# First head's probabilities turned by VectorE squares and DMA instead of TensorE, in the dilated branch and in three tiles of the forgetting branch

## The reference

```python
def forgetting_attention(q, k, v, log_f):      # branch A: 8 heads of 64
    ...
        logits = jnp.einsum('bqhd,bkhd->bhqk', qb, k) * scale
        logits = logits + (cb[..., :, None] - c[..., None, :])   # c = cumsum(log_f)
        logits = jnp.where(kpos[None, :] <= qpos[:, None], logits, -jnp.inf)
        p = jax.nn.softmax(logits, axis=-1)
        return jnp.einsum('bhqk,bkhd->bqhd', p.astype(v.dtype), v)
```

## Time and profile before

| | before |
|---|---|
| median of 3 runs | 1376.3 us (1376.18 to 1376.54) |
| the profiled execution | 1376.36 us, span 1374.6 us |
| PE, PEld, DVE, ACT, POOL busy | 1352.1, 1102.6, 741.4, 659.3, 153.2 us |
| granted TensorE clock | 0.999 |
| dilated branch, 135.9 to 406.6 | PE 266.09, DVE 186.45, ACT 177.18 us busy |
| forgetting branch, 615.4 to 843.2 | PE 225.81, DVE 99.87, ACT 119.22 us busy |

### The profile page before, as it was taken

One profiled execution on the slowest core, in us unless ns is written; L12 is line 12 of the kernel. 1 busy time (PEld: TensorE's weight loads), 2 busy tenths in 40 slices (PEclk: granted clock), 3 DMA queues, 4 the chain that ended last, 5 costly groups with the idle time before them and its releaser, 6 DMA issues.

```text
span 1374.6 us, 20906 instructions
## 1 busy us (share of the span) xinstructions
PE 1352.1 (98%) x7882; PEld 1102.6 (80%) x7882; DVE 741.4 (54%) x1675; ACT 659.3 (48%) x1430; POOL 153.2 (11%) x259
## 2 busy tenths in 40 slices
PE   7999999999999999999999999999999999999998
PEld 6988877777878888887878777787888788888886
DVE  6568866666757874574434455533333354222634
ACT  7467766666644531115454565645454422113223
POOL 3123111102112000001101012100000030000100
PEclk9999999999999999999999999999999999999999
DMA  6055222212224322323303032211322242231522
GB/s 222 24 138 131 66 66 62 69 40 64 70 50 125 88 72 67 84 90 98 93 24 93 24 101 90 66 47 55 108 62 62 62 149 67 78 84 62 185 89 102
DMA packets 114677, 114.37 MB, mean 83 GB/s; under 512 B 10609, under 2 KB 96049, under 8 KB 114321
## 3 DMA queue, kind: packets, MB, share of 16 engines
q1 hardware_dynamic: 97824, 58.22, 15.7%
q0 software_dynamic: 16752, 54.82, 12.6%
HBM read 87.37 MB, written 21.45 MB: 79 GB/s over the span
## 4 chain that ended last, share of the span: by engine, by line
PE 92%; DVE 4%; ACT 2%; issue 1%; POOL 1%; DMA 0%; POOLq 0%; ACTq 0%; DVEq 0%
PE bank L1053 22%; PE bank L1055 22%; PE bank L1054 22%; PE bank L1199 6%; PE bank L1220 6%; PE slot L1187 6%; PE slot L1053 2%; PE slot L1054 2%; PE slot L1055 2%; DVE idle_out L1586 1%; PE slot L1161 1%; DVE slot L1771 1%; DVE qc L1714 1%; PE bank L1066 0%; ACT qc L1412 0%
## 5 line engine op out<-in xcount | busy, mean ns | idle before, releaser
L1053 PE MATMUL bank<-hs,w_hl 128*128 128x512 f32 x1088 | 431.8, 397 | 3.8 <-DVE qc L1714 2.9
L1055 PE MATMUL bank<-hs,w_hl 128*128 128x512 f32 x1088 | 424.3, 390 | 0.0
L1054 PE MATMUL bank<-hs,w_hl 128*128 128x512 f32 x1088 | 423.8, 390 | 0.0
L1053 PEld LDWEIGHTS bank<-hs,w_hl 128*128 128x128 f32 x1088 | 204.3, 188 | 48.9 <-issue 8.5
L1559 DVE TENSOR_TENSOR w_hl<-w_raw,w_hl 128x512 fp32r<-128x512 f32 (+1 forms) x168 | 113.5, 678 | 235.7 <-ACT w_hl L1284 234.1
L1055 PEld LDWEIGHTS bank<-hs,w_hl 128*128 128x128 f32 x1088 | 204.1, 188 | 43.6
L1054 PEld LDWEIGHTS bank<-hs,w_hl 128*128 128x128 f32 x1088 | 204.6, 188 | 39.6
L1284 ACT ACTIVATE w_hl<-w_raw 128x512 fp32r<-128x512 f32 (+1 forms) x168 | 103.9, 621 | 161.6 <-PE bank L1055 154.1
L1586 DVE TENSOR_SCALAR_CACHE_REDUCE idle_out<-score,state 128x768 uint8<-128x768 f32 (+3 forms) x140 | 115.3, 824 | 4.8
L1771 DVE CUSTOM_DVE_ANT_0 slot<-slot,score 128x128 f32<-128x128 f32 (+5 forms) x64 | 47.0, 786 | 75.4 <-PE slot L1187 75.4
L1468 ACT ACTIVATE idle_out<-score,state 128x896 bf16<-128x896 f32 x64 | 70.0, 1093 | 10.0 <-DVE state L1582 8.8
(11 more groups left out here) (320 smaller groups left out, 2211.2 us busy)
## 6 DMA issues: line engine op xcount, KB each, us to landing
w_raw<-in_w_in_dram SPq DMA_DIRECT2D x136, 256.0 KB, 2.9
merged_scratch<-ms POOLq DMA_DIRECT2D x16, 512.0 KB, 3.5
ms<-merged_scratch POOLq DMA_DIRECT2D x16, 512.0 KB, 3.8
xn<-in_x_dram SPq DMA_DIRECT2D x8, 512.0 KB, 6.8
iq_st<-iq_hl POOLq DMA_DIRECT2D x32, 128.0 KB, 2.8
w_raw<-in_w_o_dram SPq DMA_DIRECT2D x16, 256.0 KB, 3.7
v_scratch<-vtc POOLq DMA_DIRECT2D x6, 512.0 KB, 3.0
vc<-v_scratch POOLq DMA_DIRECT2D x24, 128.0 KB, 3.8
```

The source lines that it names most:

```text
L1053: pe.matmul(out_, wh, mh, start=start, stop=False)
L1054: pe.matmul(out_, wh, ml, start=False, stop=False)
L1055: return pe.matmul(out_, wl, mh, start=False, stop=stop)
```

## The change

The plan marks runs whose head 0 goes by DMA (`by_dma`): all but the last run of the dilated branch, and channels 0 to 2 of the forgetting branch. For these, ACT computes the exponentials of head 0 first, in a new step "square" that stands ahead of the turn; DVE transposes the 32x32 squares of PR in place; POOL stores them to DRAM and loads them in four DMAs into one of two new buffers PTQ; the turn has the blocks of head 1 alone; pv reads head 0 from PTQ. pv comes two steps behind as before in the dilated branch, and three behind in the marked channels of the forgetting branch. A marked run's turn is not cut by logits. The dilated branch's PT ring has two groups instead of four. ACT waits for the former square's store before it writes PR of head 0, and POOL for the pv two squares back before it loads.

```diff
+SQUARED = ("c", "a", )
+LAG = {"c": 2, "a": 3, "b": 2}
+PTS = {"c": 2, "a": 4, "b": 4}
...
+        by_dma = [r[0]["br"] in SQUARED and s + 1 < n and (r[0]["br"] == "c" or r[0]["ch"] + 1 < NCH["a"])
+                  for s, r in enumerate(runs)]
...
-            between = 1 <= s < n and runs[s - 1][0]["slots"] == 2
+            between = 1 <= s < n and runs[s - 1][0]["slots"] == 2 and not by_dma[s - 1]
...
-            if s >= 2:
+            late = LAG[runs[0][0]["br"]]
+            due = [r for r in range(max(s - 3, 0), min(s, n)) if r + (late if by_dma[r] else 2) == s]
+            for r in due:
                 pv = ring()
...
+            if s < n and by_dma[s]:
+                step("square", unit=runs[s][-1], n=len(squares), before=squares[-2] if len(squares) > 1 else None)
...
-                parts = [(x["b"], hh, c) for x in runs[s - 1] for hh in range(2) for c in range(x["W"] // P)]
+                parts = [(x["b"], hh, c) for x in runs[s - 1] for hh in range(1 if x["dma"] else 0, 2)
+                         for c in range(x["W"] // P)]
...
+        PTQ = {"c": [at(k, f"ptsc{k}", [P, 4, P]) for k in (58, 60)], "a": [at(k, f"ptsa{k}", [P, TB, P]) for k in (44, 76)]}
...
@@ POOL @@
+                elif kind == "square":
+                    pool.wait_ge(squared, n + 1)
+                    if n >= 2:
+                        pool.wait_ge(square_in, 64 * (n - 1))
+                    pool.dma_start(mid[0:W // P].rearrange("b p c -> p b c"),
+                                   PR[br][:, 0, 0:W].rearrange("p (b c) -> p b c", c=P)).then_inc(square_stored, 16)
+                    if a["before"] is not None:
+                        full(pool, a["before"]["pv"])
+                    pool.wait_ge(square_stored, 16 * (n + 1))
+                    for j in range(4):
+                        pool.dma_start(PTQ[br][n % 2][32 * j:32 * j + 32, 0:W // P, :].rearrange("a b (i c) -> a (b i) c", i=4),
+                                       mid[0:W // P, :, 32 * j:32 * j + 32].rearrange("b (i a) c -> a (b i) c", i=4)
+                                       ).then_inc(square_in, 16)
...
@@ PE, ahead of pv @@
+                        if a["dma"]:
+                            pe.wait_ge(square_in, 64 * (a["square"] + 1))
...
@@ ACT @@
+                elif kind == "square":
+                    if a["n"]:
+                        act.wait_ge(square_stored, 16 * a["n"])
+                    act.wait_ge(logit_ready, u["L"][0] + 1)
+                    for x in u["run"]:
+                        ins = A(PR[x["br"]][:, 0, x["col"]:x["col"] + x["W"]], slot_of(x, 0)[1], ACTF.Exp, bias=mx,
+                                scale=-1.0, accum_out=dn)
+                    ins.then_inc(slot_free if u["slots"] == 2 else single_exp, 1)
...
-                    for hh in range(2):
+                    for hh in range(1 if a["dma"] else 0, 2):
...
@@ DVE @@
+                elif kind == "square":
+                    v.transpose(PR[u["br"]][:, 0, 0:W], PR[u["br"]][:, 0, 0:W]).then_inc(squared, 1)
```

More of the change, by code:

```diff
@@ L55 @@
 RATE_B = 0.84
-PTS = 4
+SQUARED = ("c", "a", )
+LAG = {"c": 2, "a": 3, "b": 2}
+PTS = {"c": 2, "a": 4, "b": 4}
 RELUS = 3
@@ L223, in pair_run @@
         n = len(runs)
+        by_dma = [r[0]["br"] in SQUARED and s + 1 < n and (r[0]["br"] == "c" or r[0]["ch"] + 1 < NCH["a"])
+                  for s, r in enumerate(runs)]
+        for run, dma in zip(runs, by_dma):
+            for x in run:
+                x["dma"] = dma
         defer[0] = True
@@ L243, in turn @@
                 step("turn", unit=run[0], groups=groups)
-            between = 1 <= s < n and runs[s - 1][0]["slots"] == 2
+            between = 1 <= s < n and runs[s - 1][0]["slots"] == 2 and not by_dma[s - 1]
             if s < n and not between:
                 logits()
-            if s >= 2:
+            late = LAG[runs[0][0]["br"]]
+            due = [r for r in range(max(s - 3, 0), min(s, n)) if r + (late if by_dma[r] else 2) == s]
+            for r in due:
                 pv = ring()
-                for x in runs[s - 2]:
+                for x in runs[r]:
                     x["pv"] = pv
                     plan.append(("pv", x))
+            if s < n and by_dma[s]:
+                step("square", unit=runs[s][-1], n=len(squares), before=squares[-2] if len(squares) > 1 else None)
+                for x in runs[s]:
+                    x.update(square=len(squares), single=sum(y["slots"] == 1 for y in squares))
+                squares.append(runs[s][-1])
             if 1 <= s <= n:
-                parts = [(x["b"], hh, c) for x in runs[s - 1] for hh in range(2) for c in range(x["W"] // P)]
+                parts = [(x["b"], hh, c) for x in runs[s - 1] for hh in range(1 if x["dma"] else 0, 2)
+                         for c in range(x["W"] // P)]
                 groups = [dict(parts=parts[g0:g0 + 4]) for g0 in range(0, len(parts), 4)]
@@ L677, in hybrid_layer_kernel @@
         v_stored, v_in = sem("v_stored"), sem("v_in")
+        single_exp, squared, square_stored, square_in = sem("single_exp"), sem("squared"), sem("square_stored"), sem("square_in")
+        square_dram = [nc.dram_tensor(f"square_scratch_{i}", [TB, P, P], F32, kind="Internal").ap() for i in range(2)]
         v_dram = [nc.dram_tensor(f"v_scratch_{i}", [P, T], F32, kind="Internal").ap() for i in range(2)]
@@ L1213, in _ @@
                         first = a["b"] // 2 * 2
-                    at_part = {part: (grp["tp"] % PTS, j) for grp in a["groups"] for j, part in enumerate(grp["parts"])}
+                    at_part = {part: (grp["tp"] % PTS[a["br"]], j) for grp in a["groups"] for j, part in enumerate(grp["parts"])}
                     for c in range(n):
                         for hh in range(2):
-                            t, j = at_part[a["b"], hh, c]
+                            if a["dma"] and hh == 0:
+                                turned = PTQ[a["br"]][a["square"] % 2][:, a["col"] // P + c, :]
+                            else:
+                                t, j = at_part[a["b"], hh, c]
+                                turned = PT[a["br"]][:, t, j, :]
                             cols = slice(HD * hh, HD * hh + HD)
                             values = V["b"][:, c, :] if a["br"] == "b" else V[a["br"]][a["ch"] % 2][:, first + c, cols]
-                            ins = pe.matmul(bank[a["pv"][0]][cols, out], values, PT[a["br"]][:, t, j, :],
+                            ins = pe.matmul(bank[a["pv"][0]][cols, out], values, turned,
                                             start=c == 0, stop=c == n - 1)
@@ L1429, in _ @@
                         full(act, a["held"]["groups"][-1]["use"])
-                    for hh in range(2):
+                        if a["held"]["dma"] and not a["dma"]:
+                            act.wait_ge(square_stored, 16 * (a["held"]["square"] + 1))
+                    for hh in range(1 if a["dma"] else 0, 2):
                         act.wait_ge(logit_ready, a["L"][hh] + 1)
```

21 lines of the change are left out of this document (16 added, 5 removed).

## The result

The changed kernel takes 1411.0 us (median of 4, 1408.8 to 1416.1) against 1376.35: a ratio of 1.0257, interval 1.0228 to 1.0286. The profiled execution took 1408.83 us, span 1407.0. It is slower by 34.6 us, where 3 us less were forecast, and outside the range. Of all executions in this document one, of the kernel of e5, ran at a granted clock of 0.558 from end to end and took 2203.5 us, where the other four of that kernel took 1380.8 to 1388.7.

What follows compares the result with a forecast made beforehand. TensorE (PE), busy 1352.1 of 1374.6 us, was taken to bound the kernel. The sum was 1376.36 + 4.6 (dilated branch) - 7.6 (forgetting branch) = 1373.4 us, own range 1370 to 1377, full range 1363 to 1384.

Steps and rivals of the forecast that it cites:

- Part 1: Both branches: head 0's transposes leave PE, saving 11.0 us dilated and 12.8 us forgetting, less 0.7 us for logits.
- Part 2: Squares on DVE: 0.62 us each at 512 columns, delaying L1714 in the dilated branch by 11.4 us, covered in the forgetting branch.
- from 3.6 to about 19: Dilated stage: sign of being right, PE idle before projection matmuls rising to about 19 us, released by L1714.
- the nine: Dilated steps where DVE's delay reaches PE: two in each of channels 1 to 4, one in channel 5; 11.4 us.
- 11.4 - (11.0 - 4.2): Dilated branch sum: DVE delay less PE's saving outside the waiting steps, giving +4.6 us, slower.
- Part 3: DMA by POOL: cost 0 in the dilated branch; forgetting branch 3 us for last values, 1.5 us for late exponentials.
- Cost 0: Dilated branch: POOL's square DMA and the store ACT waits for, hidden within two steps (22 us), some 4 us left.
- 0.5 us more per step (ACT held by a count or by a late store): Dilated branch's slow bound: extra delay in the waiting steps, the branch losing 9 us instead of 4.6.
- the last channel's wait: Forgetting branch: PE waits 3 us (ends 0 and 4.5) for the last channel's values behind the last square's loads.
- The gating of the exponential: Forgetting branch: head 1's exponential, behind one turn's evictions, makes PE wait 0.3 us x 5 = 1.5 us (0 to 4).
- POOL's queue is late: Rival, both branches: square's store, awaited by ACT, stands behind former square's loads; 1390 us, about 1382 halfway; chance 0.29.
- Strided loads: Rival: square loads as slow as the skill's rule says, 40 squares each 5 us late, 200 us more; chance 0.01.

Runs made afterwards that it cites:

- e5: Changed kernel, dilated square behind the counts and first L1774, one buffer; forgetting channels 0 to 2 load values behind the next square's store: 1382.6 us, ratio 1.0052.
- e3: Changed kernel, DVE writing its squares straight into PTQ without DMA, values two runs behind in the forgetting branch too: 1374.0 us, ratio 0.9984.
- e7: Changed kernel with a second buffer for head 0's probabilities in the dilated branch: 1396.9 us, ratio 1.0139.
- e11: The same kernel as e5, run again for a profile at full clock: 1384.2 us, ratio 1.006.
- e6: Changed kernel, dilated: two buffers, square behind first read; forgetting: stores ahead of square and values' loads, last values' store ahead of last square's loads: 1365.0 us, ratio 0.9915.
- e8: Kernel before the change, plus three DVE transposes of an unused 128x512 buffer ahead of the counts in 24 dilated steps: 1404.6 us, ratio 1.0208.
- e12: Kernel before the change, plus one DVE transpose of an unused 128x512 buffer ahead of the counts in 24 dilated steps: 1383.2 us, ratio 1.0051.
- e9: e6 with dilated squares only in each channel's third and fourth run, the third's behind its step's last read: 1359.2 us, ratio 0.9877.

## Why the prediction was wrong, step by step

- **Part 1, right but for its size.** 72 and 180 turns are left, as said. At full clock PE's work falls by 265.9 - 256.4 = 9.5 us in the dilated stage (11.0 forecast) and 225.8 - 211.7 = 14.1 in the forgetting stage (12.1 net). (The "gross 24.1" of the text is 11.0 + 12.8 = 23.8; nothing rests on it.)
- **Part 2's duration of the square was right.** L1752 takes 0.711, 0.579 and 0.445 us for 512, 384 and 256 columns, and the next instruction starts 0.64, 0.50 and 0.37 us after it, against the 0.62, 0.49 and 0.35 of the text.
- **Part 2's mechanism was right, its price not.** Without DMA (e3) PE waits 19.0 us in the dilated stage, 15.1 more than before, and this is the "from 3.6 to about 19" of the prediction (1.4 of it, at 145.56, is in a step outside the nine). But the stage lengthened by 11.2 us, not 4.6. The sum "11.4 - (11.0 - 4.2)" has no term for PE's clock after the waits: 262.7 - 256.4 = 6.3 us. PE's smaller saving adds 1.5 us, waits 0.5 us shorter than forecast and fewer small gaps take 1.2 back.
- **Part 3 failed at "Cost 0" in the dilated branch, and this is the larger miss there.** The text holds that the store on which ACT's next exponential waits "is hidden with some 4 us left". The cover was counted from square to values; what stood uncovered was the path store, exponential, square, counts, L1774, with the values' move ahead of the store in POOL's queue. It costs 294.6 - 282.6 = 12.0 us (e7; 12.9 against e3), of which 5.7 is clock. The bound of "0.5 us more per step (ACT held by a count or by a late store)" comes to 4.5 us; the waits rose by 27.8 - 19.0 = 8.8 us over those of e3, and not evenly: 3.7 at 390.24 (5.19 against 1.46), the step of the nine that lies in channel 5, 1.3 at 294.47 (3.56 against 2.29), 1.8 at 167.23, outside the nine, where e3 has none, and 0.9 at 155.89 for a square's loads.
- **Part 3 in the forgetting branch** has the last channel's wait in its place (4.61 us at 832.89; 3 forecast, just above the upper end of 4.5). The gating of the exponential hardly shows (1.0 us). What the sum put at nothing is the wait for L1774 in channels 0 to 2: 1.46, 5.61 and 2.24 us, where ACT's eviction of the q tile stands behind an exponential that waits for the store. All waits of the stage rise by 14.7 us (2.0 to 16.7). With the clock's 7.4 us: -14.1 + 14.7 + 7.4 = +8.0, where -7.6 was forecast.
- **The rival "POOL's queue is late"** (0.29, up to 1390) named the right resource and sign. It put the former square's loads ahead of the store and gave the values' move 3 us; but with the values' loads out of the way alone (e11) the forgetting stage falls from 235.8 to 222.6 us, and with the former square's loads behind the store as well (e6) by another 5.3, so the values' move was the costlier half. The clock was not in its sum either. The sum of both stages' clock loss, 17.9 us, is over half of the 32.5 us between the two profiled executions.
- **Strided loads.** The loads of a square land 2.0 to 3.1 us after issue (medians by size, 32 to 128 KB), so this rival had no part. The rule of the Trainium skill (VectorE: DVE Perf Modes, The three transpose paths) is given there for a large innermost stride of the destination; here every piece is 128 bytes in a row at both ends, so the prediction set up a rule that this kernel does not meet, and no run here tests it.
- **What I should have done:** in the step of the earlier trace rows DVE has no gap from reduce to L1714. Any instruction placed there that waits is a wait of PE, so the question for the square was not its length but everything that can hold its semaphore.

## What to carry to other kernels

An in-order engine passes on the waits of what it is given, not only its work: before a new instruction goes ahead of something that sets the pace, follow its wait back to the end, through buffers and DMA queues. Issue stores ahead of loads and of waits in a DMA queue, give the stored buffer a second copy, and take work off the bound engine only in steps that it bounds. A wait of the bound engine can cost more than its length: here stages with waits of about 2 us and more lost a fifth to a half of their waiting time again to the clock (4.8 on 21.4 us in e7's dilated stage, 7.4 on 16.7 in the forgetting stage after the change), and an estimate should carry that as a range.

## What was not expected of the hardware

- TensorE's clock falls after some short waits and not after others of the same length. In the changed kernel matmuls at 0.43 us follow the waits of 2.56 (196.82), 5.61 (716.91) and 1.92 us (257.95, from the third matmul on); in e8 they begin two matmuls after the wait of 3.17, and in e7 a few after one of 1.80 (349.62). But in e3 a wait of 1.94 us (241.78) is followed by starts 0.23 apart, in e7 one of 2.28, in e8 one of 2.37 (210.05), and in e6 the wait of 3.08 us at 792.68 leaves the granted clock at 1.00. In the dilated stage of e12, where no wait is over 1.71 us, it stayed at 1.00. The rows first of the changed kernel, then of e7:

```profile
257.95 0.47 PE L1087 MATMUL bank<-hs,w_hl 128*128 128x512 f32 x1 [1.92 <-DVE kc L1774]
...
258.97 0.63 PE L1087 MATMUL bank<-hs,w_hl 128*128 128x512 f32 x1
```

```profile
195.56 0.47 PE L1092 MATMUL bank<-hs,w_hl 128*128 128x512 f32 x1 [2.28 <-DVE qc L1781]
...
196.55 0.39 PE L1093 MATMUL bank<-hs,w_hl 128*128 128x512 f32 x1
```

- Kernels with such waits also differ more from one execution to the next: 1408.8 to 1416.1 us after the change and 1390.0 to 1398.6 in e7, where the fastest has the highest clock, against 1383.1 to 1383.4 in e12 and 1358.9 to 1359.5 in e9, whose waits in these stages are short.
- The Trainium skill (TensorE: Matmul & The Clock Gate, HAM oscillation — how this bites in real kernels) says that idle gaps between bursts bring the lower clock back. The traces agree that they can, but its example has bursts with a long gap after each; here single waits from 1.80 us on were followed by it, in a kernel that is 96% busy, and in the two stages of the changed kernel it took 17.9 us.
- A 448 KB store from 128 partitions in 512-byte pieces landed 5.0 us after issue, a 512 KB one 3.9 (medians of six and three, forgetting stage after the change); the reason is open.
